# A four-layer transformer and two expert layers on one core: expert output rows by way of DRAM, overflow phases between the rounds, weight tiles in halves

## The reference

```python
def hierarchical_moe(hin, ...):
    g_prob = softmax(xf @ w_group + b_group)         # 4 groups, the best one is taken
    g_w, g_idx = top_k(g_prob, 1)
    e_val, e_idx = top_k(e_logits_of_that_group, 2)  # 2 of its 4 experts
    e_w = softmax(e_val)
    for e in range(16):
        hid = silu(xt @ w_gate[e]) * (xt @ w_up[e])  # 1024 -> 512
        y = y + gates[:, e:e + 1] * (hid @ w_down[e])    # 512 -> 1024
```

## Time and profile before

| | |
|---|---|
| median of 3 runs | 2774.17 us (2772.34 to 2780.5) |
| the profiled execution | 2776.21 us |
| its span in the profile | 2774.5 us |
| TensorE busy | 2630.8 us (95%) |
| VectorE, ScalarE busy | 674.6 us, 476.0 us |
| bytes on SP's queue | 470.88 MB |
| first expert layer, first gate product to last scatter | 1925.96 to 2262.10 us |
| second expert layer, the same | 2432.03 to 2762.50 us |

### The profile page before, as it was taken

One profiled execution on the slowest core, in us unless ns is written; L12 is line 12 of the kernel. 1 busy time (PEld: TensorE's weight loads), 2 busy tenths in 40 slices (PEclk: granted clock), 3 DMA queues, 4 the chain that ended last, 5 costly groups with the idle time before them and its releaser, 6 DMA issues.

```text
span 2774.5 us, 30531 instructions
## 1 busy us (share of the span) xinstructions
PE 2630.8 (95%) x12794; PEld 1945.1 (70%) x12794; DVE 674.6 (24%) x1724; ACT 476.0 (17%) x1069; POOL 32.3 (1%) x59
## 2 busy tenths in 40 slices
PE   8999999889999999999999999897999989899998
PEld 5688887768888768888778888675444457744443
DVE  1410321551042231032141042223100117300001
ACT  2320002332000232000232000121111112211111
POOL 1000000000000000000000000000000000000000
PEclk9999999989999999999999999998999999899999
DMA  9424653303475323475333474422999043189950
GB/s 356 159 96 152 267 213 144 130 31 122 152 273 212 121 107 111 154 273 224 132 122 121 152 273 182 154 91 114 418 413 423 27 185 119 61 346 417 423 207 16
DMA packets 44435, 533.67 MB, mean 192 GB/s; under 512 B 4617, under 2 KB 6978, under 8 KB 9362
## 3 DMA queue, kind: packets, MB, share of 16 engines
q1 hardware_dynamic: 32976, 470.88, 43.4%
q0 software_dynamic: 8928, 58.59, 5.6%
q10 hardware_dynamic: 2402, 2.31, 0.3%
HBM read 675.38 MB, written 6.00 MB: 246 GB/s over the span
## 4 chain that ended last, share of the span: by engine, by line
PE 89%; DVE 4%; DMA 4%; issue 3%; ACT 1%; SPq 0%; DVEq 0%; POOL 0%; POOLq 0%; ACTq 0%
PE work L399 65%; PE acc L399 22%; DMA ada_ring<-in_ada_stream 2%; PE acc L447 1%; DVE oT L1696 1%; DVE att L2119 1%; DMA bias<-bias_copies 1%; DMA bias_copies<-bias_rows 0%; DMA bias_rows<-att 0%; DVE att L1945 0%; PE work L447 0%; DMA weight_ring<-in_stream 0%; DVE att L1799 0%; DMA bias<-in_stream 0%; DVE big L1884 0%
## 5 line engine op out<-in xcount | busy, mean ns | idle before, releaser
L399 PE MATMUL work<-hT,weight_ring 128*128 128x256 f32 x3264 | 713.6, 380 | 5.7 <-DVE hT L1708 4.7
L399 PEld LDWEIGHTS work<-hT,weight_ring 128*128 128x128 f32 x3264 | 620.5, 191 | 94.0 <-issue 10.2
L399 PE MATMUL acc<-big,weight_ring 128*128 128x256 f32 x2048 | 445.5, 380 | 0.0
L399 PEld LDWEIGHTS acc<-big,weight_ring 128*128 128x128 f32 x2048 | 389.6, 190 | 56.1 <-issue 3.0
L399 PE MATMUL work<-weight_ring,big 128*64 128x512 f32 (+1 forms) x1472 | 315.3, 600 | 23.8 <-issue 19.4
L399 PEld LDWEIGHTS work<-weight_ring,big 128*64 128x64 f32 (+1 forms) x1472 | 101.2, 127 | 198.7 <-issue 198.6
L1299 ACT ACTIVATE big<-work 128x512 f32<-128x512 f32 x129 | 77.0, 597 | 634.5 <-PE work L399 603.8
L2249 DVE TENSOR_TENSOR big<-work,big 128x512 f32<-128x512 f32 x22 | 15.2, 692 | 581.3 <-PE work L399 581.3
L399 PE MATMUL work<-bias,att 128*64 128x512 f32 (+1 forms) x352 | 155.6, 595 | 0.9 <-ACT att L1299 0.9
L399 PE MATMUL work<-weight_ring,hT 128*128 128x512 f32 x288 | 132.6, 614 | 18.8 <-DMA weight_ring<-in_stream 10.6
L399 PE MATMUL work<-oT,weight_ring 128*128 128x256 f32 x640 | 145.1, 385 | 0.0
(11 more groups left out here) (262 smaller groups left out, 2229.6 us busy)
## 6 DMA issues: line engine op xcount, KB each, us to landing
weight_ring<-in_stream SPq DMA_DIRECT2D x232, 2048.0 KB
ada_ring<-in_stream SPq DMA_DIRECT2D x29, 2048.0 KB
bias<-in_stream SPq DMA_DIRECT2D x29, 2048.0 KB
ada_ring<-in_ada_stream POOLq DMA_DIRECT2D x48, 1024.0 KB, 6.9
bias_copies<-bias_rows POOLq DMA_DIRECT2D x2, 1536.0 KB, 17.2
weight_ring<-in_stream SPq DMA_DIRECT2D x2, 1024.0 KB, 8.3
resident<-in_resident SPq DMA_DIRECT2D x1, 2008.0 KB, 16.3
bias_copies<-bias_rows POOLq DMA_DIRECT2D x1, 1728.0 KB, 17.4
```

What stands on the lines that cost most here:

```text
L399: return pe.matmul(o, a, b, start=start, stop=stop, skip_group_check=True)
```

## The change

It touches the two expert layers. Five parts:

1. Outputs of all rounds but the last go to DRAM (`expert_rows`), 128 rows of 1024 values a round, by a DMA that POOL issues. At the layer's end four indirect DMAs fetch for each token the row of its first and of its second choice (`row_index`, made by VectorE). VectorE scales and adds them, 16 transposes bring them into `acc`. Rows of the last base round's two experts don't go this way: that round keeps its scatter.
2. A table `STEPS` sets the order on TensorE, ScalarE and VectorE. The three overflow rounds' phases (numbers 8, 9 and 10) stand between phases of the base rounds, and round 7 comes last. Gathers for overflow rounds go to `hT`.
3. In the expert layers a tile is loaded in two halves of 1 MB with a semaphore each. A phase uses the first halves of its tiles, then the second ones; SP may refill a half when its phase has finished with it (`half_used` or `work_full`). Down tiles are laid out so that a half holds 512 output columns.
4. The router's first matmul counts up `tile_begun`, which releases the place of the tile before the layer.
5. `rows_over_partitions`, the scatters of rounds 0 to 9 and VectorE's `spread_at` for each round are gone; VectorE has some small steps for the indices and weights instead.

```diff
+STEPS = (
+    ("gate", 0), ("up", 0), ("pick", (1, 0)), ("pick", (4, 0)), ("turn", 0), ("down", 0),
+    ("gate", 1), ("up", 1), ("pick", (1, 1)), ("pick", (4, 1)), ("turn", 1), ("down", 1), ("gate", 8),
+    ("gate", 2), ("up", 8), ("up", 2), ("pick", (2, 0)), ("turn", 2), ("down", 2), ("turn", 8), ("down", 8),
+    ("gate", 3), ("up", 3), ("pick", (2, 1)), ("gate", 9), ("turn", 3), ("down", 3),
...
+    ("gate", 6), ("up", 6), ("up", 10), ("turn", 6), ("down", 6), ("turn", 10), ("down", 10),
+    ("gate", 7), ("up", 7), ("spread", 0), ("turn", 7), ("down", 7))
...
-            def scatter(p):
-                pe.wait_ge(spread_ready, layer * ROUNDS + p + 1)
-                for m in range(KB):
-                    ins = mm(pe, accb(m), expert_out(p, m * P, m * P + P), spread_at(p), p == 0 and m in (0, 2, 4, 5), p == ROUNDS - 1)
...
+            def scatter_last():
+                for m in range(KB):
+                    mm(pe, accb(m), expert_out(LAST, m * P, m * P + P), spread_at(), False, True).then_inc(acc_full, 1)
+
+            def rows_to_blocks():
+                for tt in range(2):
+                    pe.wait_ge(combined, 2 * layer + tt + 1)
+                    for m in range(KB):
+                        pe.matmul(accb(m)[:, tt * P:tt * P + P], row_of(0, tt)[:, m * P:m * P + P], R("ident"),
+                                  start=tt == 0 and m in (0, 2, 4, 5), stop=True, is_transpose=True, skip_group_check=True)
+
+            def product(kind, p, u):
...
+                for h in range(2):
...
+                    ins = several_experts(p, w, h, wk(u), lambda k, a, b: picked(d, k, (p % 2) * P + a, (p % 2) * P + b), steps)
+                    if h == 0:
+                        ins.then_inc(half_used, 1)
+                ins.then_inc(work_full, 1)
...
+                else:
+                    wait_evacuated(pe, [units["turn", n]])
+                    for h in range(2):
+                        if n == LAST and h == 1:
+                            rows_to_blocks()
+                        pe_open(pe, u + h)
+                        steps = [(k, k == 0, k == 3, None) for k in range(4)]
+                        several_experts(n, 2, h, wk(u + h), lambda k, a, b: hiddenT(n, k, a, b), steps).then_inc(work_full, 1)
...
         def act_moe(act, st):
...
+                elif kind == "down":
+                    i = DOWNS.index(n)
+                    if i >= 2:
+                        act.wait_ge(rows_kept[i % 2], 16 * (WRITES * st.layer + i // 2))
+                    for h in range(2):
+                        act_out(act, u + h, expert_out(n, h * 512, h * 512 + 512))
...
         def dve_moe(v, st):
...
+            for tt in range(2):
+                v.wait_ge(rows_back[tt], 32 * (layer + 1))
+                own.link(v, v.tensor_scalar(row_of(0, tt), row_of(0, tt), CM("kept_w", tt, tt + 1), None, ALU.mult))
+                v.scalar_tensor_tensor(row_of(0, tt), row_of(1, tt), CM("kept_w", 2 + tt, 3 + tt), row_of(0, tt),
+                                       ALU.mult, ALU.add).then_inc(combined, 1)
...
+        def pool_rows(pool, st):
+            units = moe_table(st)
+            for i, p in enumerate(DOWNS[0:-1]):
+                wait_evacuated(pool, [units["down", p], units["down", p] + 1])
+                row = (p if p < LAST else p - 1) * P
+                pool.dma_start(moe_rows[row:row + P], expert_out(p, 0, D)).then_inc(rows_kept[i % 2], 16)
+            pool.wait_ge(index_ready, st.layer + 1)
+            for i in range(2):
+                pool.wait_ge(rows_kept[i], 16 * WRITES * (st.layer + 1))
+            for tt in range(2):
+                for c in range(2):
+                    pool.indirect_dma_start(row_of(c, tt), None, moe_rows,
+                                            bass.IndirectOffsetOnAxis(ap=row_index[:, 2 * c + tt:2 * c + tt + 1], axis=0)
+                                            ).then_inc(rows_back[tt], 16)
...
+                    if w < 2 and half_n == 0:
+                        sp.wait_ge(half_used, 2 * ROUNDS * layer + sum(o < 2 for _, o in PHASES[0:i]) + 1)
+                    else:
+                        sp.wait_ge(work_full, u + 1 + (half_n if w == 2 else 0))
...
+                several = 2 if at.spill is None else 4
+                for half_n in range(2):
+                    for n in range(several):
+                        load_half(tiles[t + n], half_n)
```

More of the change, by code:

```diff
@@ L165, in schedule @@
         add("norm2", i, unit=1, sq=8, h=1, rstd=1)
-        add("moe", i, unit=1 + 4 + 1 + 4 + 2 + 5 * ROUNDS + 4 * (DOUBLES - 1), tile=MOE_TILES, acc=1)
+        add("moe", i, unit=10 + sum(UNITS[kind] for kind, _ in STEPS), tile=MOE_TILES, acc=1)
         add("residual", i, x=1)
@@ L180, in tile_table, with add @@
     first = moes[0].at["tile"]
-    tiles, used, last_in, fixed = [], Counter(), {}, 0
+    tiles, used, twice, last_in, fixed, number = [], Counter(), Counter(), {}, 0, 0
     total = plan[-1].at["tile"]
-    spills = {st.at["tile"] + 3 * NEXP + j: (st.layer, j // 12, j % 12) for st in moes for j in range(3 * SPILL)}
-    for t in range(total):
+    def add(phase=None, spill=None, source=None):
+        t = len(tiles)
         slot = t % RING if t < first else (t - first) % (RING + 2)
         used[slot] += 1
-        tiles.append(TileAt(slot, used[slot], last_in.get(slot), None if t in spills else fixed, spills.get(t)))
-        fixed += t not in spills
+        twice[slot] += phase is not None
+        tiles.append(TileAt(slot, used[slot], twice[slot], last_in.get(slot), source, spill, number, phase))
         last_in[slot] = t
+    while len(tiles) < total:
+        layer = [i for i, st in enumerate(moes) if st.at["tile"] == len(tiles)]
+        if layer:
+            for i, (n, w) in enumerate(PHASES):
+                for j in range(2 if n < BASE else 4):
+                    spill = (layer[0], n - BASE, 4 * w + j) if n >= BASE else None
+                    add(layer[0] * len(PHASES) + i, spill, None if spill else fixed + 6 * n + 2 * w + j)
+            fixed += 3 * NEXP
+        else:
+            add(source=fixed)
+            fixed += 1
+        number += 1
     assert fixed == NTILES, fixed
@@ L1222, in several_experts @@
+                lo = t0 + sum(2 if n < BASE else 4 for n, _ in PHASES[0:at])
+                return [lo + n for n in range(2 if p < BASE else 4)]
+            def several_experts(p, w, half_n, to, lhs, steps):
                 ts = tiles_of(p, w)
                 n = P // len(ts)
-                for i, t in enumerate(ts):
-                    ins = mm(pe, to[n * i:n * i + n], lhs(n * i, n * i + n), wtile(t, k, c0, 512, width), start, stop)
-                    if begins and i < begun(p, w) or ends and i < ended(p, w):
-                        ins.then_inc(tile_begun, 1)
@@ L1289, in pe_moe @@
-            wait_evacuated(pe, [units[-1][4], units[-1][4] + 1])
-            scatter(ROUNDS - 1)
+                for t in ts:
+                    if half_n == 0:
+                        pe_tile(pe, t)
+                    else:
+                        pe.wait_ge(second_landed[tiles[t].slot], 16 * tiles[t].second)
+                for k, start, stop, ready in steps:
+                    if ready is not None:
+                        wait_evacuated(pe, [ready])
+                    for i, t in enumerate(ts):
+                        ins = mm(pe, to[n * i:n * i + n], lhs(k, n * i, n * i + n),
+                                 slot_of(tiles[t].slot, half_n * TILE // 2 + (k % 4) * 512, 512), start, stop)
@@ L1293, in act_full @@
+            wait_evacuated(pe, [units["spread", 0], units["down", LAST], units["down", LAST] + 1])
+            scatter_last()
         def act_full(act, u):
@@ new lines, in _ @@
+            t = 1
+            while t < len(tiles):
+                at = tiles[t]
+                if at.phase is None:
+                    slot_free(at)
+                    sp.dma_start(whole(at.slot), stream[at.fixed]).then_inc(landed[at.slot], 16)
+                    t += 1
+                    continue
+                if at.spill is not None and at.spill[2] == 0:
+                    layer, quad, _ = at.spill
+                    sp.wait_ge(visits_ready, layer + 1)
+                    visits = sp.value_load(visit_tile[0:1, SPILL:SPILL + 1], min_val=0, max_val=SPILL)
+                    firsts = [sp.value_load(visit_tile[0:1, 4 * quad + n:4 * quad + n + 1], min_val=0, max_val=3 * NEXP - 5)
+                              for n in range(4)]
+                several = 2 if at.spill is None else 4
+                for half_n in range(2):
+                    for n in range(several):
+                        load_half(tiles[t + n], half_n)
+                t += several
```

283 lines of the change are left out of this document (155 added, 128 removed).

## The result

| | before | changed |
|---|---|---|
| median, us (lowest to highest) | 2777.34 (2772.34 to 2791.72), 4 runs | 2732.98 (2728.03 to 2744.03), 4 runs |
| ratio, 95% interval | | 0.9844 [0.9805, 0.9883] |
| profiled execution / its span, us | 2776.2 / 2774.5 | 2734.99 / 2733.2 |
| first expert layer, us | 336.1 | 316.2 |
| second expert layer, us | 330.5 | 312.6 |

Faster by 44 us, 1.6 per cent, where 74 us were forecast: 2733 lies 33 us above the forecast of 2700 and 3 us outside the range of 2684 to 2730. Both layers are longer than the 310 us that the prediction named as a sign of being wrong. The spans agree with the layers: 2774.5 - 2733.2 = 41.3 us, of which the layers give 19.9 and 17.9 and the stretch up to the first gate product 3.0 (1925.96 to 1922.96).

What follows compares the result with a forecast made beforehand. Base rounds run at the weight stream's pace with TensorE nearly as busy; overflow rounds are bound by TensorE. Each layer 290.6 + 4 + 1.5 = 296.1 us, saving 40.0 and 34.4: 2774.2 - 74.4 = 2700 us, range 2684 to 2730.

Steps and rivals of the forecast that it cites:

- Work and turns, 290.6 a layer: Each expert layer without waits for data: work 276.8 us, turn waits 12.1, last-round waits 1.7, sum 290.6 us.
- The halves' rate: Expert-layer weight halves stream at 427 GB/s, landing one after another at 2.45 us each and 2.6 us late.
- A rule against the halves: Slower expert-layer weight stream: 412 GB/s by queue shares, 5 us more in total; by the skill's rule, 2760 us.
- rival 1: Expert-layer halves stream slower, at 377 GB/s, with weight waits of 13 and 19 us: 2724 us, chance 0.12.
- The spread overflow phases: Overflow work among base rounds fills the holes: queue share about 0.85 over the whole layer, no empty stretch.
- Weights, 4 us a layer: Phase-by-phase waits for weight halves: 3.3 and 4.3 us, taken as 4 per layer, tightest at up 3 and up 7.
- The tail, 1.5 us: DRAM way at the layer's end: 15.3 to 29 us against 20.1 of TensorE work, stall taken as 1.5 per layer.
- The upper bound: DRAM way at the layer's end with the bias pieces' issue and landing times: 29 us, a stall of 9.
- Rival 2: Layer-end gathers land late or share engines with next stage's tiles: stalls 5 to 9 us per layer, 2707 to 2715, chance 0.14.
- The clock: The main sum for the expert layers held no term for TensorE's clock slowing behind waits.
- Rival 3: Short turn waits in both layers each lower TensorE's clock, about 1.7 us lost each, 37 us: 2737, chance 0.05.
- Rivals 4 and 5: Layer-end gathers in series at 14.4 us each: 2795, chance 0.05; interleaved overflow steps leave the stream standing: 2741, chance 0.05.

Runs made afterwards that it cites:

- e1_no_rows: The changed kernel without the row writes, the four gathers and all waits for them (layers' outputs wrong): 2696.99 us, ratio 0.9728.
- e3_block: The changed kernel with overflow rounds 8, 9, 10 in one block between rounds 6 and 7, some gathers moved along: 2752.65 us, ratio 0.9911.
- e11_spaced: The changed kernel, steps reordered: turns covered, overflow phases singly behind one to three base phases, rounds overlapping: 2703.01 us, ratio 0.9756.
- e9_alone: The changed kernel with SyncE asking for up 7's tiles only when the layer's four gathers have landed: 2764.63 us in one run.
- e6_covered: The changed kernel, steps reordered: something between each turn and its down product, down 6 last before round 7: 2705.53 us, ratio 0.9763.
- e7_late_next: The changed kernel with the next stage's first tile asked for only after the second token half's gathers have landed: 2735.33 us, ratio 0.9847.

## Why the forecast was wrong, point by point

- **Work and turns, 290.6 a layer: right.** e1_no_rows has 289. A turn with its idle takes 1.3 us where I took 1.54: the idle is 0.7, not the 0.94 of the earlier trace rows.
- **The halves' rate: right, within 2 per cent.** 425 GB/s at a share of 1.02 from 2075 to 2090, as the whole tiles had the earlier trace rows; over the run the queue's engine time gives 470.89 MB / (0.451 x 2733.2 us) = 382 GB/s against 391 before: 2 of the 3.5 per cent of "A rule against the halves", and far from the 12 of rival 1. The Trainium skill's rule in "SBUF — State Buffer", The DMA setup-cost knee, some 330 to 340 GB/s for 1 MiB, is not borne out for queued halves.
- **The spread overflow phases: right in direction.** The empty stretch is gone, and e3_block shows 6 to 9 us a layer for it.
- **Early release of the tile before the layer: right as far as seen.** The 1.81 us wait at the first up is gone. That the layer starts 3.0 us earlier is not shown to come from it, since this start moves by more between executions.
- **Weights, 4 us a layer: the step that failed, with the next.** It was 11.9 and 14.2. Where halves stand close, half a base phase is 3.5 us of TensorE and two halves, 4.9 us of stream: each waits 1.4 us once the places held by overflow phases have used up the lead (1.29, 1.33 in the timeline), and 2.2 to 2.6 with a write's 1.2 us on top (2.23). There every byte more is a wait: ten writes brought 7.8 and 5.6 us of waits, the next ten 8.4 and 7.2. The stretch that the prediction worked out, up to up 3's second half, shows it. Its rows: SyncE's eight halves and POOL's writes, from issue, and the chain for the last of the eight:

```profile
2018.87 12.65 SPq L2421 DMA_DIRECT2D weight_ring<-in_stream  x8
...
2023.44 0.53 POOL L2372 DMA_DIRECT2D expert_rows<-oT  x1 [40.32 <-ACT oT L1350]
2031.80 0.53 POOL L2372 DMA_DIRECT2D expert_rows<-oT  x1 [7.83 <-ACT oT L1350]
...
2031.04 13.62 DMA weight_ring<-in_stream
```

The eighth half landed at 2044.66, 25.8 us behind the first one's issue, where 23.4 was counted. The working had one row write in this stretch, and two were issued (of down 2 and down 8), 1.2 us; the other 1.2 is a later landing or a slower rate, which the rows don't tell apart. TensorE waited 3.5 us there (2.23 and 1.29) and not about 1. My sum let nearly all of the writes fall into slack: its 3.3 and 4.3 us, writes included, are what e1_no_rows has without any. Prices fitted after the first runs (2.42 us for a half, 3.4 to its landing, 1.9 for a write or gather, in the expectation of e11_spaced) bring the same sum near the waits, but they are fitted, not measured: of a write's own price the trace leaves open whether it is above 1.2, since the engines move 387 GB/s in the stretch with two writes (2020 to 2035) but 394 in one without (1995 to 2005), against 425 elsewhere.
- **The tail, 1.5 us: the other step that failed.** The waits were 10.7 and 3.3. I took 3.8 us for the write's landing and 5.0 for the last gather's, "on POOL's queue, which was empty there". Alone they are 2.9 and 6.0 (e9_alone), so these prices were fair. But the 16 DMA engines are shared, and they were full (2206 to 2226, share 1.02) with the halves of round 7, one behind the other, and the next stage's tiles. Landings became 8.6 and 19.1. That the four places of down 10 caused the crowding, by holding these halves back, is not shown: with down 6 there instead (e6_covered) the last gather still took 17.4 and 16.1 us. Issuing was priced too short as well: 2202.76 to 2206.59 and 0.94 is 4.8 us, not 2.1. The upper bound didn't reach it either: the terms shown for it (0.6 + 0.5 + 3.8 + four issues of 0.95 + 14.4 + 3.3) give 26.4 us and not the 29 stated, and from the end of down 10 to the combined rows it was 35.7. Rival 2 named the shared engines, though with the next stage's tiles (4 us of it, e7_late_next) and not with the larger part, round 7's own halves.
- **The clock: 0 in the sum.** 316.2 - 288.8 - 11.9 - 10.7 leaves 4.8 us, and 312.6 - 289.2 - 14.2 - 3.3 leaves 5.9. Most of it is the clock: TensorE's busy time, each microsecond times what the granted clock lacks to 1.00, comes to 4.0 and 5.0 us. The clock was 0.50 for the first 4.5 us of work behind the 9.54 us wait, and from 2164 to 2167 behind the 3.11 us one; in the second layer it fell behind waits of 2.08, 2.52 and 2.24 us. The 2.23 us wait at 2039.85 left it at 1.00. e1_no_rows has no wait for weights above 1.3 us and 1.00 throughout both layers. Rival 3 had it the wrong way round: the idles of 0.7 us cost no clock, the waits that I had not counted did.
- **Rivals 4 and 5: did not come.** The gathers overlap, in a queue with nothing else all four are there 6.0 us after the last issue.

Two steps failed, then: the writes that were to fall into slack, and landings taken from an empty queue; the clock came behind their waits. Weights (8 to 10 us a layer), tail (2 to 9) and clock (5 to 6) make 39.8 us in the two layers; work and turns were 3.2 us under the forecast, and the layers miss it by 36.6. The stretches outside them became 3.5 us shorter, which was not forecast and which no run explains: that leaves the missing 33, and it is luck that the number is not further off. The three things had been rivals, and each range was priced as if the others stayed out.

## What to carry to other kernels

A transfer's landing time from a stretch with empty queues holds only for such a stretch: before a new transfer is put on the critical path, ask which loads come free at the same moment, because all queues share the engines (6.0 us against 19.1 here). In a stream with hardly any slack, bytes are priced at the stretch with the least of it, not at the mean. And where a step is removed, look at what it covered: here a pick, a gate or another round's turn in its place, with the last rounds exchanged, brought another 0.8 per cent of the time before (0.9763 against 0.9844, e6_covered).

## What the runs showed of the hardware that I had not expected

- The same 0.5 MB row write lands in 2.9 to 3.7 us with the weight stream held back (e9_alone) and in 8.4 to 8.6 us beside a full stream; the last of four gathers of 128 rows of 4 KB in 6.0 to 6.1 us there and in 15.9 and 19.1 us in the change.
- An indirect DMA keeps POOL 0.94 to 1.00 us and 0.30 us to the next, against 0.53 us for a plain one.
- Idles of 0.7 us before the down products, eleven in each layer of e1_no_rows, leave TensorE's granted clock at 1.00. In the change it fell to 0.50 within the wait of 9.54 us and behind waits of 2.08 to 3.11 us, but not behind those of 2.23 us at 2039.85 and 2.19 us at 2527.02.
